# First products of four stages begun in the stage before, and gathers that wait for their group's gates

## What is computed

```python
mod = silu(c) @ w_ada + b_ada                      # 6 x 1024 numbers
h = rmsnorm(x, g_norm1) * (1.0 + scale1) + shift1
aq, ..., gl = split(h @ w_in)                      # 8448 columns
...                                                # four mixers: ya, yb, yc, yd (512 wide each)
branches = einsum('bsgc,gcd->bsgd', stack([ya, yb, yc, yd], axis=2), w_branch)
mixed = sum(sigmoid(gl) * branches, axis=2) @ w_o
x = x + gate1 * mixed
h2 = rmsnorm(x, g_norm2) * (1.0 + scale2) + shift2
q = (h2 @ w_q).reshape(T, 8, 2, 128)
s = einsum('thpd,pnd->thpn', q, sub_keys)          # scores against 2 x 128 keys
...                                                # top 16 of 128^2 experts for each head and token
act = gelu(einsum('cd,chkd->chk', xc, u_experts[ic]))
out = einsum('chk,chkd->cd', gc * act, v_experts[ic])
x = x + gate2 * out
```

## Time and profile before

| | before |
|---|---|
| time, median of 3 runs | 1990.13 us (1989.17 to 1999.84) |
| profiled execution | 1993.8 us, span 1991.7 |
| TensorE busy | 1864.4 us, 94% |
| weight loads | 1628.8 us, 82% |
| VectorE busy | 1531.2 us, 77% |
| GpSimd busy | 793.3 us, 40% |
| ScalarE busy | 723.2 us, 36% |
| granted clock of TensorE, mean | 0.978 |
| HBM traffic | 524.7 MB, 263 GB/s over the span |

### The profile page before, as it was taken

How to read it: one execution, slowest core, us unless ns; L and a number is a source line. 1 busy time by engine, 2 the same in 40 slices (tenths; PEclk the granted TensorE clock), 3 DMA queues, 4 the chain that set the end, 5 groups by cost and what they waited for, 6 DMA issues and landing times. The chain is left out here.

```text
span 1991.7 us, 27792 instructions
## 1 busy us (share of the span) xinstructions
PE 1864.4 (94%) x10096; PEld 1628.8 (82%) x10096; DVE 1531.2 (77%) x2272; ACT 723.2 (36%) x970; POOL 793.3 (40%) x488
## 2 busy tenths in 40 slices
PE   5899979999898798988999999999979999999997
PEld 4788857777787787988999989999858888888886
DVE  6656458775445567999995499999868889888988
ACT  2322234444423222322333355666523333332331
POOL 1000088000042000567777777878534434333330
PEclk9999989999998899999999999999989999999999
DMA  8699478879483240659999989999999999999993
GB/s 299 207 310 331 144 186 228 250 216 276 143 283 83 57 95 21 155 134 261 260 255 269 258 237 309 308 318 309 341 385 391 391 391 390 391 391 390 392 391 123
DMA packets 305205, 526.21 MB, mean 264 GB/s; under 512 B 20282, under 2 KB 210283, under 8 KB 300524
## 3 DMA queue, kind: packets, MB, share of 16 engines
q1 hardware_dynamic: 268268, 391.10, 64.5%
q0 software_dynamic: 36864, 134.23, 19.3%
HBM read 438.75 MB, written 85.99 MB: 263 GB/s over the span
## 5 line engine op out<-in xcount | busy, mean ns | idle before, releaser
L123 PE MATMUL u_s<-h_hi,u_hi 128*128 128x384 f32 x1024 | 353.4, 345 | 20.4 <-POOL u_lo L1870 19.0
L125 PE MATMUL u_s<-h_hi,u_lo 128*128 128x384 f32 x1024 | 344.6, 337 | 0.0
L124 PE MATMUL u_s<-h_lo,u_hi 128*128 128x384 f32 x1024 | 344.2, 336 | 0.0
L123 PE MATMUL v_o<-v_v_hi,v_w_hi 128*128 128x512 f32 x768 | 301.2, 392 | 17.3 <-DVE v_w_lo L2124 13.0
L124 PE MATMUL v_o<-v_v_lo,v_w_hi 128*128 128x512 f32 x768 | 300.7, 392 | 0.0
L125 PE MATMUL v_o<-v_v_hi,v_w_lo 128*128 128x512 f32 x768 | 300.5, 391 | 0.0
L1870 POOL TENSOR_TENSOR u_lo<-u_ut,u_hi 128x1024 fp32r<-128x1024 f32 x79 | 198.8, 2517 | 94.4 <-ACT u_hi L1650 94.0
L123 PEld LDWEIGHTS u_s<-h_hi,u_hi 128*128 128x128 f32 x1024 | 193.7, 189 | 32.3 <-POOL u_lo L1870 25.7
L124 PEld LDWEIGHTS u_s<-h_lo,u_hi 128*128 128x128 f32 x1024 | 193.8, 189 | 0.0
L125 PEld LDWEIGHTS u_s<-h_hi,u_lo 128*128 128x128 f32 x1024 | 193.4, 189 | 0.0
L123 PEld LDWEIGHTS v_o<-v_v_hi,v_w_hi 128*128 128x128 f32 x768 | 145.4, 189 | 48.2 <-DVE v_w_lo L2124 13.4
(11 more groups left out here) (334 smaller groups left out, 4089.3 us busy)
## 6 DMA issues: line engine op xcount, KB each, us to landing
u_raw<-in_u_experts_dram SPq DMA_DIRECT2D x160, 256.0 KB, 5.9
v_raw<-in_v_experts_dram SPq DMA_DIRECT2D x74, 512.0 KB, 12.3
v_slot<-in_v_experts_dram SPq DMA_DIRECT2D x54, 512.0 KB, 12.7
expert_acts<-u_ao SPq DMA_DIRECT2D x64, 384.0 KB, 5.2
u_raw<-turned_experts SPq DMA_DIRECT2D x96, 256.0 KB, 8.5
expert_gates<-u_gs SPq DMA_DIRECT2D x12, 2048.0 KB, 11.2
v_gt<-expert_gates SPq DMA_DIRECT2D x30, 768.0 KB, 15.2
w_in_raw<-in_w_in_dram SPq DMA_DIRECT2D x17, 1024.0 KB, 11.8
```

The costliest lines, as they stand in the source:

```text
L123: nc.tensor.matmul(out, w[0], x[0], start=first, stop=False)
L124: nc.tensor.matmul(out, w[0], x[1], start=False, stop=False)
L125: return nc.tensor.matmul(out, w[1], x[0], start=False, stop=last)
```

## The change

There are six parts.

1. *Conditioning.* VectorE now does block 0, half of block 1, block 2, and six of the eight steps of block 3 (`OWN_ROWS = 2`). TensorE does the other half of block 1 and two rows of block 3, into columns of the same accumulator bank (`p_own`). The subtraction for the first weight block moves from GpSimd to VectorE, ahead of the coefficients. Loads, products and exponential of the `lam` vectors move later. At the end TensorE does `first_product(..., 0)`: 48 matmuls over the first 256 tokens. `phase_project` begins with `first_product(..., 1)`, the other 256 tokens, into the same two accumulator banks, which now live over both stages (`acc_w`, with the semaphore `mm`).
2. *Gates to output projection.* In the last branch ACT and VectorE also split three of the four blocks of `w_o`; the last two sums move from GpSimd to VectorE (`sum_ok`); the last piece is split in two halves. Then TensorE does six of eight chunks (`SEAM`) for two blocks of the first token tile. `phase_out` splits the fourth block alone.
3. *Output projection to queries.* During token tile 2 ACT and VectorE split the first block of `w_q`; after the last transposes TensorE does its first 256 tokens (`first_queries(..., 0)`), `phase_query` the rest. Block 2 of `w_q` is requested after that product instead of after the first block's split, block 3 after the first requests for experts.
4. *End of the queries.* ACT takes the last queries before the two expert tiles.
5. *Semaphores.* `phase_mix` hands on a larger range of used semaphores; `lo_ok` of the queries counts one less per block.
6. *Last stage.* GpSimd waits before each group's gathers for that group's gates, which are alternately `gt_in0` and `gt_in1`.

```diff
@@ phase_condition
+def first_product(nc, acc, parts, keep, half, done=None):
+    hs = slice(half * 2 * P, (half + 1) * 2 * P)
+    for m in range(2):
+        for c in range(KD):
+            ms = slice(m * P, (m + 1) * P)
+            ins = three(nc, acc[m][:, hs], (parts[:, 0, c, ms], parts[:, 2, c, ms]), (keep["h_hi"][:, c, hs], keep["h_lo"][:, c, hs]), c == 0, c == KD - 1)
+        if done is not None:
+            ins.then_inc(done, 1)
...
-            pool.wait_ge(w_hi_ok, 1)
-            pool.wait_ge(blk_ok, 1)
-            nc.gpsimd.tensor_tensor(w_parts[:, 2], raw[0][:, :, :], w_parts[:, 0].bitcast(F32), ALU.subtract).then_inc(w_lo_ok, 1)
...
-            for b in (0, 2, 3):
+            for b, upto, rows_of in ((0, S, KD), (1, S // 2, KD), (2, S, KD), (3, S, KD - OWN_ROWS)):
...
+            dve.wait_ge(w_hi_ok, 1)
+            dve.wait_ge(blk_ok, 1)
+            nc.vector.tensor_tensor(w_parts[:, 2], raw[0][:, :, :], w_parts[:, 0].bitcast(F32), ALU.subtract).then_inc(w_lo_ok, 1)
+            dve.wait_ge(mod_mm, 1)
...
+            for c in (2, 3):
+                for x in range(KD):
+                    ins = nc.tensor.matmul(p_mod[:, 4 + c:5 + c], ring[1][:, x, c * P:(c + 1) * P], keep["csil"][:, x:x + 1], start=x == 0, stop=x == KD - 1)
+            pe.wait_ge(acc_c.sem, 2 * KD)
+            shares((0, 1, 2, 3, 4, 5)).then_inc(blk_ok, 1)
+            pe.wait_ge(acc_c.sem, 3 * KD)
+            shares((8, 9, 10, 11))
+            pe.wait_ge(ada_last, 16)
+            for c in range(12, 16):
+                for x in range(KD - OWN_ROWS, KD):
+                    nc.tensor.matmul(p_own[:, c - 12:c - 11], ring[3][:, x, c % 4 * P:(c % 4 + 1) * P], keep["csil"][:, x:x + 1], start=x == KD - OWN_ROWS, stop=x == KD - 1)
+            pe.wait_ge(acc_c.sem, 4 * KD - OWN_ROWS)
+            ins = shares((12, 13, 14, 15))
...
+            pe.wait_ge(w_lo_ok, 1)
+            pe.wait_ge(low_ok, 2)
+            first_product(nc, acc_w, w_parts, keep, 0)
@@ phase_project
-            for b in range(4):
+            first_product(nc, acc, parts, keep, 1, mm)
+            for b in range(1, 4):
                 product(b, b, b < 2)
@@ phase_gate, ScalarE
+                if d < GATED_BLOCKS:
+                    nc.scalar.activation(wo_hi[d][:, :, :], w_o[:, :, d * BW:(d + 1) * BW], ACT.Copy).then_inc(sem["wo_hi_ok"], 1)
@@ phase_gate, VectorE
+                if d < GATED_BLOCKS:
+                    out_low(d)
+
+            def last_sum(m):
+                weigh(NBR - 1, 3, False, (m,))
+                dve.wait_ge(sem["part_ok"], 2 * (4 * NBR - 1) + m + 1)
+                nc.vector.tensor_tensor(merged[:, 6 + m, :], merged[:, 6 + m, :], part[m][:, :], ALU.add).then_inc(sem["sum_ok"], 1)
@@ phase_gate, TensorE
+            pe.wait_ge(sem["wo_lo_ok"], 2)
+            for c in range(SEAM):
+                pe.wait_ge(sem["m_lo_ok"], c // 2 + 1)
+                for b in range(2):
+                    three(nc, acc[b][:, 0:BW], (m_hi[:, c, 0:P], m_lo[:, c, 0:P]), (wo_hi[b][:, c, :], wo_lo[b][:, c, :]), c == 0, False)
@@ phase_out
+                if i == 2:
+                    dve.wait_ge(sem["q_hi_ok"], 1)
+                    nc.vector.tensor_tensor(q_lo[:, :, :], q_raw[0][:, :, :], q_hi[:, :, :].bitcast(F32), ALU.subtract).then_inc(sem["q_lo_ok"], 1)
...
             transposes(TT - 1)
+            pe.wait_ge(sem["q_lo_ok"], 1)
+            pe.wait_ge(sem["x2_ok"], NB * TT)
+            pe.wait_ge(sem["low_ok"], 2)
+            first_queries(nc, acc, q_hi, q_lo, keep, 0)
@@ phase_query
+            sp.wait_ge(sem["mm"], 2)
+            load_queries(sp, a, raw[0], w_in[0], 2)
             ahead(sp)
+            sp.wait_ge(sem["lo_ok"], 1)
+            load_queries(sp, a, raw[1], w_in[1], 3)
...
             queries(PH - 2, 0)
+            queries(PH - 1, 1)
             for t in range(2):
                 act.wait_ge(tiles["ut_ok"], t + 1)
                 nc.scalar.activation(tiles["hi"][t][:, :, :], tiles["ut"][t][:, :, :], ACT.Copy).then_inc(tiles["hi_ok"], 1)
-            queries(PH - 1, 1)
@@ last stage
-            pool.wait_ge(sem["gt_in1"], 16)
             for g in range(1, NG):
+                pool.wait_ge(sem[f"gt_in{g % 2}"], 16 * (g // 2) + 16 * (g % 2))
```

More of the change, by code:

```diff
@@ L1294, in _, with first_queries @@
             transposes(TT - 1)
+            pe.wait_ge(sem["q_lo_ok"], 1)
+            pe.wait_ge(sem["x2_ok"], NB * TT)
+            pe.wait_ge(sem["low_ok"], 2)
+            first_queries(nc, acc, q_hi, q_lo, keep, 0)
+def first_queries(nc, acc, hi, lo, keep, half, done=None):
+    hs = slice(half * 2 * P, (half + 1) * 2 * P)
+    for m in range(2):
+        ms = slice(m * P, (m + 1) * P)
+        for c in range(KD):
+            ins = three(nc, acc[m][:, hs], (hi[:, c, ms], lo[:, c, ms]), (keep["h_hi"][:, c, hs], keep["h_lo"][:, c, hs]), c == 0, c == KD - 1)
+        if done is not None:
+            ins.then_inc(done, 1)
 def load_queries(sp, a, raw, w_in, b):
```

207 lines of the change are left out of this document (111 added, 96 removed).

## The result

The changed kernel takes 1967.4 us (median of 4 runs, 1965.83 to 1968.06) against 1989.65 us before (4 runs): a ratio of 0.9874, with a 95% interval from 0.9856 to 0.9892. The forecast was 1953.5 us, with a range of 1947 to 1968, so the way was right and the gain was 22 us where 36.6 were expected. In the profiled executions the span went from 1991.7 to 1965.6 us, by 26.1.

What follows compares the result with a forecast made beforehand. TensorE was taken to bound the kernel, so only its waits and lower-clock stretches could give time: 9.8 + 7.1 + 6.6 + 3.1 + 10 = 36.6 us off 1993.8 gives 1957.2, for the median 1953.5 us; range 1947 to 1968.

Steps and rivals of the forecast that it cites:

- the rival in which the seams shift their work: Stage borders: a stage ends with its slowest engine, now TensorE at the lower clock; total gain 23 us, 1967 us; chance 0.10.
- The first border: Conditioning to input projection: coefficients ready at about 40.3 instead of 45.4, half-width matmuls begun early; gain 9.8 us (6 to 10).
- The second border: Gates to output projection: weights split and products begun in the last branch; gain 7.1 us (5.2 to 8.4).
- the late end of 3.5 us: Last branch: GpSimd's sums wait out VectorE's splits, the last product starts 3.5 us late; gain there 5.2 instead of 7.1.
- The third border: Output projection to queries: half the first query product follows the transposes early; gain 6.6 us (4 to 8).
- Block 2 of the weights is requested 4.4 us later: Queries: its landing, some 7 us, is covered by a whole product; without that cover it costs up to 4.
- End of the queries: ACT's last queries moved ahead of two expert tiles, for which it waited 13.9 us; gain 3.1 us (2 to 3.5).
- Last stage: Gathers wait for their group's gates; five instead of 13 go first, TensorE's 13.0 us wait falls to 2.2; gain 10 (3 to 13).
- the rival of the wrong stall: Last stage: a late value tile, not the gates, sets the 13 us stall; gain 1 to 2, 1962 us; shares 0.22.
- that slack doesn't shrink over 29 groups: Last stage: weights ready 2.4 us ahead in the tightest case, without drift; reason for leaning to the upper side of 3 to 13.
- DMA bounds the last stage: Last stage: transfers at 391 GB/s limit it, gain there 3, total 29.6, 1960.5 us; chance 0.22, shared with the wrong stall.
- The rival with waits for gathered rows in every group: Last stage: the gathers' wait is paid in every group, 2 us in each of 29; slower, 2021 us; chance 0.03.

## Why the prediction held, and where it did not

The measured 1967.4 us lies 0.6 us inside the upper bound of 1968, and that bound was the sum of the rival in which the seams shift their work. This rival did not come: it gave the borders 13 us, and they gave 25.7. So the forecast was right in its way and in its borders; that its range held in spite of the last stage is luck.

**The first border** (9.8 expected, 11.2 measured) went by the steps named: the split took 2.29 us on VectorE, the coefficients came at 39.4 for 40.3 forecast, the second product of the projection began at 59.8 for 61.2, and the projection lost nothing to its transfers, which was the doubt behind the lower bound. Of the two halves of the argument the overlap was found in a run, with 6.2; the coefficients are the 5.0 that remain, of which a run shows 2.7.

**The second border** (7.1 expected, 7.5 measured): from the first product of the gates to the last it takes 96.2 us in place of 95.1, so VectorE's three splits cost TensorE 1.2 us at most: its wait ahead of the last piece grew by 0.8 (0.93 to 1.74), and over all profiles this stretch varies from 95.1 to 96.1 without the splits and from 95.5 to 97.0 with them. That lies at the lower end of the 0.3 to 3.5 that were allowed for, below the 2 taken. The rows of GpSimd and VectorE above fit to 0.2 us with operations that go strictly one after another: GpSimd's first sum to 590.7, VectorE's `merged_lo` to 591.8, GpSimd's second sum to 593.0, VectorE's split of 2.3 to 595.1. The rule of the Trainium skill ("SBUF — State Buffer", section "SBUF: two separate sides") says this, and the trace agrees; but the late end of 3.5 us that was derived from it did not come. That the loop of VectorE, GpSimd and ScalarE had slack there is the likely reason; no run isolates it.

**The third border** (6.6 expected, 5.4 measured): the half product, the transposes and the clock went better than forecast, the second product beginning 7.6 us earlier counted from the end of the output projection. The step that failed is "Block 2 of the weights is requested 4.4 us later". It was the only transfer that the forecast followed past SP. Block 3 stands behind eight requests for experts there, kept ScalarE waiting for 9.46 us, and cost 2.2 us of the 7.6. The change had said so in its diff; the forecast read the list of SP as far as block 2.

**End of the queries** (3.1 expected, 1.6 measured between the two kernels, 4.2 by the run that undoes it alone): TensorE's first product of the experts begins 57.3 us after the third scores in place of 60.5, 3.2 earlier, as forecast, and 1.6 us went to the clock behind it, which no term held.

**Last stage** (10 expected, 3 as lower bound, 1.1 measured, so below the term's own bounds). Two steps of this term were right: with fewer gathers ahead of them the gates of group 2 were multiplied 29.2 us behind the stage's first product in place of 40.6 (11.4 earlier, 10.8 forecast), and a wait of 1.84 us was left in that place for 2.2 forecast. GpSimd issued five gathers, from 1424.07 to 1430.8, and then waited for these gates; the value tile that ScalarE got only at 1484 came along (32.9 us behind the first product in place of 44.3), so the rival of the wrong stall is answered too. Two costs were missed: the next group was late in turn (its value tile came last, after GpSimd had issued ten gathers in one go for group 2), and TensorE stood another 4.3 us, and with two waits in place of one it fell to the lower clock twice.

```profile
1444.04 2.40 POOL L1395 DMA_INDIRECT v_acc<-in_u_experts_dram,few_idx  x1 [13.24 <-DMA v_gt<-expert_gates]
...
1470.13 1.06 ACT L2148 ACTIVATE v_v_hi<-v_raw 128x1024 fp32r<-128x1024 f32 x1 [16.36 <-DMA v_raw<-in_v_experts_dram]
```

By the run without the wait TensorE stood 6.1 us longer (17.4 in all against 11.3), but its part of the stage was only 3.3 longer; the other 2.8 go with the lower clock (by the pitch of the matmuls it cost 6.2 us over the head with the wait and 3.2 without). The step that failed is the slack. It was read off as "2.4 us, all that TensorE could advance", "that slack doesn't shrink over 29 groups", and so the upper side was chosen. The slack did not shrink because both went at the same pace: TensorE at 16.3 us a group (the trace has 72 matmuls of 512 columns in a group, 0.227 us each, and not the 96 of the description above), the queues at 6.38 MB a group, which are 16.3 us too at 391 GB/s. That left nothing to give. In the changed kernel the slack does shrink: the weights are ready 2.0 to 2.5 us ahead of TensorE in groups 8 to 12 and 0.8 to 1.4 in groups 27 to 30. The last weights came 516.4 us behind the first product in place of 517.1, since the same 200 MB had to come first. Nor was TensorE's end the end: VectorE's list behind the last weights needs 34.5 us, and before the change TensorE was later than this list by only 0.6 us. TensorE did advance, by 4.9 us, and 3.7 of it became tail.

The rival "DMA bounds the last stage" was the right one, at 22 in 100, with 3 us where there was 1; its 1960.5 us is nearer to 1967.4 than the forecast. (The seam rival's 1967 is nearer still, by chance.) It said that a string of small waits for `v_w_lo` after 1500 us would prove it, and there was none: the bound showed in the tail, for which the forecast had no term. The rival with waits for gathered rows in every group did not come. GpSimd does wait in each group now, though, for the gates:

```profile
POOL rows_buf L1395 <- DMA v_gt<-expert_gates: 98.4, 14, 20.5
POOL v_acc L1395 <- DMA v_gt<-expert_gates: 97.2, 14, 13.2
```

195.6 us of waits on GpSimd cost nothing, since the queues stay full (391 GB/s in both kernels).

What stays open is the experts' stage, 1.2 us longer after, with waits for `u_lo` of about 1 us in other places; that it varies from 631.7 to 638.6 over these profiles speaks for chance. The difference between 26.1 in the profiles and 22 in the medians is of that size too. Why the mixers take 264 to 267 us in most profiles and 270 in three was not followed.

## What to carry to other kernels

Before a stall in a long stage is booked as a gain, ask what each other full resource needs from the stage's first instruction to the end: here the transfers (up to the last weights) plus VectorE's list behind them came to within 1 us of TensorE's whole path, so removing 6 us of TensorE's stalls gave 1. A steady slack between two resources says that their rates are equal, and not that there is room. To see whether a removed stall is worth anything, relieve the suspected second bound and run the edit with and without: in the stage it was 8.2 us against 1.0 here, and 3.3 against 1.0 in the medians.

At a border between stages, beginning the next product early can save twice, as work done and as a clock that doesn't fall. It was worth 6.2, 6.5 and 4.0 us here for products of 5.7, 4.3 and 5.7: clearly more than the work at the second border, less than the work at the third. And where requests are moved on a queue, follow every one that now stands behind others, not just the first.

## What was not expected

- VectorE and GpSimd in the last branch take strict turns: 1.22 us operations show as 1.94, a split of 2.29 as 3.37, two sums of 2.54 as 3.52. The lengths in a profile hold the time spent standing.
- The clock of a stretch depends on what came just ahead: shortening a gap moved the half clock from sixteen small score products to twelve expert products, and 1.6 us of a gain of 3.2 with it.
- The first matmuls of the half product in the conditioning started 0.21 us apart from 46.5 to 50.4 us and 0.12 apart behind it, the two pitches that elsewhere go with 0.50 and 1.00, while the profile gives the granted clock as 1.00 in both windows:

```profile
46.00:51.00 5.00, 5.00 (x27) 5.00 (x28) 3.77 (x10) 4.94 (x8) 0.00 (x0) 1.00 0.01 3
51.00:56.00 5.00, 4.70 (x39) 4.53 (x38) 0.38 (x3) 1.92 (x2) 0.00 (x0) 1.00 0.17 36
```

By the pitch the clock was low in the first of them; that rests on the pitch alone, and no run here tells it from another cause. Either way the matmuls took the longer time, and in the first 60 us it is their pitch that is to be priced.
